# A decoder block with product-key retrieval: the second tail's residual, norm and queries taken one tile, then two, with a new pace and two waits moved

## The reference

```python
def reference(...):
        y = hybrid_mixer(h, ...)                 # ends in (g_attn * attn + g_conv * conv) @ w_out
        x = x + gate1 * rms_norm(y, g[1])        # residual step
        h = rms_norm(x, g[2]) * (1.0 + scale2) + shift2   # second norm
        y = peer_ffn(h, ...)
        x = x + gate2 * rms_norm(y, g[3])

def peer_ffn(h, w_q, sub_keys, expert_down, expert_up):
    q = (h @ w_q).reshape(B, S, PEER_HEADS, 2, PEER_HALF)        # queries
    s1, s2 = q . sub_keys                                        # scores, 128 per half
    v1, i1 = lax.top_k(s1, 16); v2, i2 = lax.top_k(s2, 16)
    top, ci = lax.top_k(v1[..., :, None] + v2[..., None, :], 16) # 8 heads x 16 experts a token
    expert = ea * 128 + eb; gate = softmax(top)
    pre = einsum('td,tkd->tk', h, expert_down[expert])           # 128 rows of 2048 a token
    act = gelu(pre) * gate
    return einsum('tk,tkd->td', act, expert_up[expert])          # 128 rows more
```

## Time and profile before

| what | value |
|---|---|
| time, median of 3 runs | 4117.74 us (4116.97 to 4125.35) |
| profiled execution: its time, its span | 4122.73 us, 4120.9 us |
| mean granted TensorE clock | 0.768 |
| busy in the span: PE, DVE, ACT, POOL | 2794.8, 2276.4, 544.5, 1410.1 us |
| moved by DMA | 1430.07 MB, mean 347 GB/s |

### The profile page before, as it was taken

One profiled execution on the slowest core, in us unless ns is written; L12 is line 12 of the kernel. 1 busy time (PEld: TensorE's weight loads), 2 busy tenths in 40 slices (PEclk: granted clock), 3 DMA queues, 4 the chain that ended last, 5 costly groups with the idle time before them and its releaser, 6 DMA issues.

```text
span 4120.9 us, 38729 instructions
## 1 busy us (share of the span) xinstructions
PE 2794.8 (68%) x15652; PEld 1651.8 (40%) x15652; DVE 2276.4 (55%) x3525; ACT 544.5 (13%) x1207; POOL 1410.1 (34%) x1109
## 2 busy tenths in 40 slices
PE   5999899899898999998878443443444434444435
PEld 3787788789754555554755110110100101101101
DVE  6399779742554333335754566654665564444442
ACT  3211221200210111111211111010101100100000
POOL 2421211000013344333134554435434435444342
PEclk9999999999999999999989555555555555555556
DMA  9353323798558999989889999999999999999998
GB/s 367 145 225 122 154 104 141 269 408 331 208 207 338 386 403 378 410 343 385 339 332 420 385 404 421 422 421 421 421 421 417 421 421 415 420 422 420 421 422 369
DMA packets 204145, 1430.07 MB, mean 347 GB/s; under 512 B 24640, under 2 KB 24768, under 8 KB 32192
## 3 DMA queue, kind: packets, MB, share of 16 engines
q0 software_dynamic: 152064, 1107.36, 65.2%
q1 hardware_dynamic: 45984, 308.30, 19.3%
q10 hardware_dynamic: 5920, 11.94, 0.8%
HBM read 1420.13 MB, written 7.39 MB: 346 GB/s over the span
## 4 chain that ended last, share of the span: by engine, by line
PE 40%; DMA 38%; DVE 13%; POOL 4%; issue 3%; ACT 2%; ACTq 0%; another core or an unknown queue 0%; DVEq 0%; SPq 0%; POOLq 0%
PE psum L621 40%; DMA front<-in_down,back 28%; DMA front<-in_up,back 8%; DVE front L1633 4%; POOL front L592 3%; DVE back L1400 2%; DMA front<-in_w_conv_o 1%; DVE back L1369 1%; ACT back L1158 1%; POOL x_low L576 1%; DMA back<-in_x 1%; DVE back L1734 0%; ACT front L1262 0%; DVE back L1569 0%; DVE back L1563 0%
## 5 line engine op out<-in xcount | busy, mean ns | idle before, releaser
L621 PE MATMUL psum<-front 128*32 128x512 f32 (+3 forms) x7120 | 1383.3, 615 | 855.5 <-DMA front<-in_up,back 789.2
L1633 DVE CUSTOM_DVE_ANT_0 front<-front,back 128x2048 f32<-128x2048 f32 x512 | 1170.8, 2292 | 1318.0 <-DMA front<-in_down,back 1150.0
L621 PEld LDWEIGHTS psum<-front 128*128 128x128 f32 (+1 forms) x7120 | 626.4, 162 | 1546.4 <-issue 1327.2
L592 POOL DMA_INDIRECT front<-in_down,back x512 | 603.7, 1179 | 909.7 <-DVE back L1633 665.0
L621 PE MATMUL psum<-back,front 128*32 128x128 f32 (+3 forms) x4400 | 641.3, 459 | 351.2 <-DMA back<-in_up,back 172.7
L592 POOL DMA_INDIRECT front<-in_up,back x442 | 526.3, 1191 | 941.3 <-PE psum L621 891.4
L621 PEld LDWEIGHTS psum<-back,front 128*32 128x32 f32 (+1 forms) x4400 | 374.3, 168 | 627.4 <-issue 348.4
L570 POOL TENSOR_TENSOR w_low<-front,w_high 128x2048 fp32r<-128x2048 f32 x33 | 155.2, 4704 | 539.4 <-ACT w_high L1046 539.4
L621 PE MATMUL psum<-x_high,w_high 128*128 128x512 f32 x640 | 252.6, 395 | 9.2 <-POOL x_low L576 6.4
L621 PE MATMUL psum<-x_high,w_low 128*128 128x512 f32 x640 | 251.0, 392 | 0.0
L621 PE MATMUL psum<-x_low,w_high 128*128 128x512 f32 x640 | 250.9, 392 | 0.0
(11 more groups left out here) (161 smaller groups left out, 1676.3 us busy)
## 6 DMA issues: line engine op xcount, KB each, us to landing
front<-in_w_in SPq DMA_DIRECT2D x116, 1024.0 KB, 5.0
back<-in_ada_w SPq DMA_DIRECT2D x64, 1024.0 KB, 7.9
front<-in_w_q SPq DMA_DIRECT2D x48, 1024.0 KB, 4.8
front<-in_ada_rows POOLq DMA_DIRECT2D x32, 1024.0 KB, 13.7
front<-in_w_out SPq DMA_DIRECT2D x32, 1024.0 KB, 4.9
front<-in_w_conv_o SPq DMA_DIRECT2D x16, 1024.0 KB, 16.1
front<-in_w_attn_o SPq DMA_DIRECT2D x16, 512.0 KB, 11.6
front<-in_down,back POOLq DMA_INDIRECT x512
```

The lines of the kernel that those rows point to most:

```text
L592: nc.gpsimd.indirect_dma_start(out=row_, out_offset=None, in_=table[:, :], in_offset=bass.IndirectOffsetOnAxis(ap=idx4[:, t % 2, c:c + 1], ...
L621: return nc.tensor.matmul(o, a, b, start=start, stop=stop)
L1633: V.tensor_tensor_reduce(d_row[s], d_row[s], h2r, 1.0, 0.0, ALU.mult, ALU.add, pre[:, b // 16 % 2, b % 16:b % 16 + 1]).then_inc(dots_done, 1)
```

## The change

The second tail's chunk order becomes "out", x of tile 1, queries of tile 1, x of tiles 2 and 3, queries of tiles 2 and 3. The residual step, second norm and the scaled h are made for tile 1 alone, then, behind tile 1's queries and routing, for tiles 2 and 3 together. `PACE` spreads blocks 0 to 127 over fewer chunks: it stands at 124 at the end of "out", at 128 in the first two query groups of tile 1, and ends at 168 instead of 156. `WIDE` goes from 160 to 176, and the routing of tiles 2 and 3, which runs beside the tile before, begins 44 blocks into that tile in steps of 20 instead of 28 and 24. Tile 0's last exponential on ACT now stands ahead of the second tail's first sigmoids, and DVE's gates that use it stand behind block 3's dot instead of ahead of block 0's.

```diff
 def tail_groups(c):
-    out += [("out", i, 4) for i in range(4)] + [("x", t, 1) for t in range(TAIL[c][1] // P)]
-    for go, _, _ in QUERIES[c]:
+    out += [("out", i, 4) for i in range(4)]
+    for go, q0, qn in QUERIES[c]:
+        out += [("x", t, 1) for t in range(q0 // P, (q0 + qn) // P)]
         out += [(kind + go, i, k) for i in range(4) for kind, k in (("q", 4), ("sc", 0))]
...
-WIDE = 160
+WIDE = 176
+ROUTE, STRIDE = 44, 20
...
 def block_pace():
     work = [k * (12 if kind in ("ga", "gc", "co", "out") else 6 if kind == "ao" else 9 if kind == "x" else 4) / max(k, 1)
-            for kind, _, k in tail_groups(1) for _ in range(k)][:-16]
+            for kind, _, k in tail_groups(1) for _ in range(k)][:-30]
     out = [round(128 * at / sum(work)) for at in itertools.accumulate(work)]
-    return out + [128 + 7 * (i + 1) // 4 for i in range(16)]
+    out += 4 * [128] + [129, 130, 131, 132, 133, 135, 136, 138]
+    return out + [141, 144] + [144 + 3 * (i + 1) // 2 for i in range(16)]
...
             def tail(c):
                 for cg in range(4):
                     passed(c, 3)
+                    if c == 1 and cg == 0:
+                        gate_exp(0, 3)
                     for m in range(4):
                         act.wait_ge(g_done, DONE[c, "ga", cg] + m + 1)
...
-                    if c == 1 and cg == 0:
-                        gate_exp(0, 3)
...
+                    if b == 3:
+                        gates(0, 3)
...
+                for go, q0, qn in QUERIES[c]:
+                    goes, tq = c + (go != ""), slice(q0, q0 + qn)
+                    row_, wide = row[:, q0 - t0:q0 - t0 + qn], [P, 4, qn]
+                    for i in range(4):
+                        y_ = hT[:, 4 * i:4 * i + 4, tq]
+                        st.did(V.tensor_tensor(y_, y_, row_.unsqueeze(1).to_broadcast(wide), ALU.mult))
...
+                    for i in range(4):
+                        passed(c, 4)
+                        if not go:
+                            dve.wait_ge(act_took, ATOOK[c, "sc", i] + 4)
+                            for step in range(6):
+                                route(c, i, step)
+                            if i:
+                                gates(c, i - 1)
+                    if c and not go:
+                        gates(c, 3)
```

More of the change, by code:

```diff
@@ L552, in _ @@
                         behind(c)
[L553 to L556, removed]
+                for _, q0, qn in QUERIES[c]:
+                    for t in range(q0 // P, (q0 + qn) // P):
+                        put(x_row, x[t * P:(t + 1) * P, :])
+                        behind(c)
                     for i in range(4):
@@ L938, in squares @@
                     for i in range(count):
-                        ins = mm(ps[:, 6, 0:n], ones, buf[:, i, 0:n], first and i == 0, last and i == count - 1)
+                        ins = mm(ps[:, 6, 0:buf.shape[2]], ones, buf[:, i, :], first and i == 0, last and i == count - 1)
                     return ins
@@ L979, in tail @@
                 pe.wait_ge(act_took, ATOOK[c, "out", 3] + 4)
[L980 to L997, removed]
-                for go, q0, qn in QUERIES[c]:
+                squares(sqt[:, :, 0:n], 4, False, True).then_inc(ss_done, 1)
+                for go, q0, qn in QUERIES[c]:
+                    goes = c + (go != "")
+                    tiles = range(q0 // P, (q0 + qn) // P)
+                    for t in tiles:
+                        r = x_row[chunk_in()]
+                        for m in range(4):
+                            if t > tiles[0]:
+                                pe.wait_ge(dve_took, VTOOK[c, "x", t - 1] + m + 1)
+                            elif go:
+                                pe.wait_ge(act_took, ATOOK[c, "sc", 3] + m + 1)
+                            for k in range(4):
+                                ins = nc.tensor.transpose(ps[:, m, k * P:(k + 1) * P], r[:, (4 * m + k) * P:(4 * m + k + 1) * P], ident)
+                            ins.then_inc(g_done, 1)
+                        chunk_out(c)
+                    for kk in range(8):
+                        pe.wait_ge(sq2_ready, 8 * goes + kk + 1)
+                        ins = squares(sqt[:, 2 * (kk % 2):2 * (kk % 2) + 2, 0:qn], 2, kk == 0, kk == 7)
+                        ins.then_inc(sqs_used if kk < 7 else ss_done, 1)
+                    pe.wait_ge(h2_ready, KT * (goes + 1))
+                    pe.wait_ge(keys_in, 16 * (c + 1))
                     for i in range(4):
@@ L1008, in tail @@
                             group(4, 4, hT, plain, act_took, ATOOK[c, "sc" + go, i - 1], None, tq, scores)
-                        elif go:
-                            group(4, 4, hT, plain, act_took, ATOOK[c, "sc", 3], None, tq, scores)
                         else:
-                            group(4, 4, hT, plain, dve_took, VTOOK[c, "x", n // P - 1], None, tq, scores)
+                            group(4, 4, hT, plain, dve_took, VTOOK[c, "x", tiles[-1]], None, tq, scores)
             tail(0)
@@ L1670, in retrieve @@
                         unit_act(unit)
[L1671 to L1673 removed]
+                    if b == 3:
+                        gates(0, 3)
+                    t, at = b // 128 + 1, b % 128 - ROUTE
+                    if 2 <= t < TT and 0 <= at < 4 * STRIDE:
+                        n, step = at // STRIDE, at % STRIDE
                         if step % 2 == 0 and step < 12:
                             route(t, n, step // 2)
[L1676 removed]
+                        if step == 18:
                             gates(t, n)
@@ L1739, in tail @@
-                dve.wait_ge(std2_ready, 2 * c + 2)
-                dve.wait_ge(dve_took, VTOOK[c, "x", n // P - 1] + 4)
-                st.link(V.reciprocal(row[:, 0:n], row[:, 0:n]))
-                for i in range(4):
-                    V.tensor_tensor(hT[:, 4 * i:4 * i + 4, tok], mixT[:, 4 * i:4 * i + 4, tok],
-                                    row[:, 0:n].unsqueeze(1).to_broadcast(wide), ALU.mult).then_inc(h2n_ready, 1)
-                for i in range(4):
-                    passed(c, 4)
-                    dve.wait_ge(act_took, ATOOK[c, "sc", i] + 4)
-                    for step in range(6):
-                        route(c, i, step)
-                    if i:
-                        gates(c, i - 1)
```

70 lines of the change are left out of this document (35 added, 35 removed).

## The result

The changed kernel took 4097.9 us in the median of four runs (4095.6 to 4112.2), the kernel before 4119.6 us beside it: a ratio of 0.9949, 95% interval 0.9926 to 0.9973. It is faster by some 22 us, where 45 were forecast (4120 to 4075). The first profiled execution was the longest of its four (4112.2 us); against the other profile it came 4.9 us later to the second tail and lost 8 us more from there on.

The account below looks back on a forecast made before the run. DMA standing idle between retrieval's first dot and the end was taken as what counts, with TensorE limiting some stretches. Gains of 45 - 5 + 6 = 46 us gave 4075 us, from 4120; range 4045 to 4110.

Parts of the forecast that it names:

- A: 1163 to 1290 us, the two moved waits: TensorE's 15.2 us wait nearly gone, standing DMA 23 us instead of 46.5.
- the sum: All stretches' gains added: 45 - 5 + 6 = 46 us; includes 14 us from moved waits and "out" ending 5 us later.
- B: 1290 to 1900 us, up to the end of "out": ten more blocks fit, standing DMA 29 us instead of 50.6.
- the rate above 400 named as a sign: DMA rate up to the end of "out" should exceed 400 GB/s if the ten extra blocks fill idle time.
- The rival that the fill fails: Before the end of "out" 50.6 us stay standing, 21.6 us of gain lost: 4097 us, chance 0.19.
- C: Residual step in two parts, between "out" and "q2": DMA stands 53 us against 47.7, so -5 us.
- first: Stop of retrieval before tile 1's first routing: 61.5 us, 42 us of transfers in flight, 19 us idle.
- second and third: Stops around tile 1's second and third routings and gates: 5 us for the restart and 2 us idle.
- fourth: Stop at six dots, tile 1's fourth routing, gates, scaling and x tile: 50 us, 34 us covered, 16 idle.
- fifth: Stop during the second chain, up to the first "q2" chunk: 38 us, 27 us covered, 11 idle.
- The slower rival: Residual-step stops covered by nothing but buffers: 127 us standing instead of 53, time 4150 us, chance 0.09.
- E: 2275 to 2400 us, slot widening moved from block 160 to 176: standing DMA 7 us instead of 12.5, so +6.

Follow-up runs that it names:

- the second profile: The changed kernel run again unchanged for another profile, against the kernel before: 4100.4 us, ratio 0.9955; profiled execution 4099.2 us, span 4097.4.
- the two edits: Slots widened at block 168, and dots up to block 141 directly behind tile 1's fourth routing; added to the changed kernel: 4088.9 us, ratio 0.9922 to the kernel before.
- run 22: Not a follow-up run: the words say that the rows of `up` come 22 blocks behind those of `down`; no kernel or time belongs to them.
- its best descendant: Changed kernel with slots at 168, dots behind tile 1's fourth routing and four TensorE rows inside the second chain: 4086.1 us, ratio 0.9921 to the kernel before.
- the fastest version: Kernel before with moved waits, faster table, one-piece residual step, slots at 168 and dots up to 141 behind tile 1's fourth routing: 4078.5 us, ratio 0.9897.

## Why the prediction was right, and where it was wrong

**A: right.** The moved waits gave what their rows said, with TensorE's wait gone: 28.0 us of A left by the waits alone, 17.8 with the table, 23 forecast. Alone they give 20 us of time (ratio 0.9950; 15.6 us between the two profiles, counted from the fourth routing), where the sum had 14.

**B: right in kind, its size open.** The rate rose from 387 to 399 GB/s with ten more blocks in the stretch (396 in the first profile), and 33.2 or 37.6 us stand where 29 were forecast; the rate above 400 named as a sign was not reached. PE was through with "out" at 1906.4 us in the second profile and 1918.0 in the first, against 1907.5 before. Counted from the fourth routing that is 2 and 9 us later, where the sum had 5. The rival that the fill fails gave 4097, the measured time to a microsecond, but by a mechanism that did not occur: it needed B to stay at 387. Read as a limit, the Trainium skill's 358 GB/s for a core ("DMA: Bandwidth & Descriptors", Specifications) fails with it: 399 GB/s flowed over 610 us here.

**C: the term that failed**, -5 forecast and -24.8 measured. By stop, forecast and measured: first 19 and 24.6; second and third 7 and 4.3; fourth 16 and 21.4; fifth 11 and 21.8. The places were right, and so were the transfers counted for the last two: 24.5 forecast, and 25.2 MB in 2041 to 2144 (261 and 226 GB/s), which is 24. Wrong was the length, 88 us forecast and 103.5 measured (2040.1 to 2143.6). Two pieces make that up. The dots ahead of the fourth routing waited for their rows, so the first x tile was done 56.7 us after 2040.1 instead of 50. And I took the first "q2" chunk's start for the end of the fifth stop: that came after 35.4 us (PE at 2132.2), near the 38 forecast, but the gathers go on only when PE has made that chunk and a row behind it, 11 us later:

```profile
2132.23 35.25 PE L625 MATMUL psum<-front 128*128 128x256 f32 x160 [11.76 <-ACT front L1271]
```

```profile
2130.00:2135.00 5.00, 2.77 (x7) 2.23 (x8) 2.00 (x2) 3.68 (x7) 0.00 (x0) 0.50 0.00 0
2135.00:2140.00 5.00, 5.00 (x17) 4.15 (x16) 0.00 (x0) 0.00 (x0) 0.00 (x0) 0.68 0.00 0
```

Part of these 11 us is the clock, which I had left out: PE had waited 11.8 us for ACT, and the granted clock is 0.50 (1.2 GHz) in the first of the two rows of stretches, 0.68 in the second and 1.00 from 2140 on. At 1.00 the same work would have taken some 3 us less (an estimate: half of 2.8 us and a third of 5). The six dots inside the chain, which the list shows and I did not price, lie in those 35.4 us. In the first stop 15.4 transfers were in flight where I had counted 17.

Behind the sizes lies the step that failed. I priced the table's gain in B and the stops in C apart, and did not ask what the same ten blocks had covered before. The pair of the waits alone and the waits with the table answers it: 29 us gained in A and B, 24 lost in C, with no split at all. My sentence "The split shortens the first stop and makes a new one" is right, but the two do not add up to a gain: 0.9949 and 0.9955 with it, 0.9942 without. With the two edits added it is 0.9922 with it, 0.9897 without; these intervals still touch, so that the split costs time is likely and not shown. The slower rival's mechanism, stops covered by little but the buffers, is what happened in part: C at 74.6, short of the 107 from which it would have decided.

**E: wrong in sign**, +6 forecast, -1.4 measured. "At 176 the slot's last user is 174, and no meeting falls there" looked at the widening alone. The rows of `up` run 22 blocks behind those of `down`, so with the widening at 176 they have three slots up to position 198, and the meeting at 192 falls into that time: 289 GB/s in 2425 to 2450, and 420 with 168. The three slots "cost nothing by themselves" only where there is no meeting.

**What stays open.** Why the executions of the split versions scatter by some 20 us (4095.6 to 4116.0 for the changed kernel, 4078.8 to 4098.5 for its best descendant) while the four of the fastest version lie within 7; the kernel before, whose residual step is in one piece too, spreads over 15 us in the 43 executions beside the experiments (4112.8 to 4128.1), so the split need not be the reason. And how much of the fastest version's gain is the slots' and how much the dots'.

## What to carry to other kernels

When work is taken ahead to fill an idle stretch, look up what it covered where it stood, and price both stretches in one sum; the shortest way is an experiment that moves the work and nothing else. A stop is over only when the engine that frees the buffer has come past its next piece of work, not when its wait ends. And a change of several parts should be run part by part: here the two moved waits alone gave as much as the whole, and no pair of versions shows a gain from the structural part.

## What the runs showed of the hardware

With nearly nothing but gathers in flight, 420 GB/s flowed over 200 us of a stage in which the number of slots changes (2250 to 2450 of the fastest version). With the query weights among them it was 409 GB/s from 2097 to 2144 of the same version and 420 from 2100 to 2275 before, and 398 beside 587 us of TensorE work in 610. The long stops were times in which GpSimd waited for DVE or PE, 27.7 to 31.7 us each in the list above. The granted TensorE clock does not tell the versions apart, 0.77 on average in the runs at 4097.4 and at 4074.2 us alike, but it was at 0.50 when PE began the first "q2" chunk behind the second chain. And profiled executions of versions that do the same work up to there reach the same instruction, the fourth routing, at times between 1147.7 and 1155.5 us, and two executions of the changed kernel at times 4.9 us apart, so a difference of some microseconds between two single profiles says nothing until both are counted from such a point.
